# A hybrid mixer block on one core: pairs of delta tiles in 18 beats instead of 19, the first pair a beat sooner, the last tiles in another bank

## The chip, the cores and the metric

The kernel runs on one core of a Trainium2 chip. TensorE (PE) multiplies matrices into the eight banks of PSUM; VectorE (DVE), ScalarE (ACT) and GpSimd (POOL) do the rest; SyncE (SP) issues most DMAs. Each engine works off its own instructions in order and waits on semaphores that the others raise. The metric is the time of one execution in microseconds (us), the median of several runs; lower is better.

## The reference

One decoder layer of width 1024 over 1024 positions, batch 1: a modulated norm, one input projection into three causal mixers (GLA with 4 heads, mLSTM with 4 heads, gated DeltaNet with 8 heads), sigmoid merge gates, an output projection, then a modulated norm and a SwiGLU of width 2816, and a last norm. All is float32. The change is in the DeltaNet mixer, whose chunks of 64 rows need the inverse of a triangular matrix:

```python
kk = jnp.einsum('bhnid,bhnjd->bhnij', kc, kc)
a_mat = jnp.where(causal_mask(c, strict=True), beta[..., :, None] * kk * gamma, 0.0)
t_mat = a_mat + jnp.eye(c)
u = triangular_solve(t_mat, vc * beta[..., None])
w = triangular_solve(t_mat, kc * (beta * jnp.exp(cum))[..., None])
a_qk = jnp.einsum('bhnid,bhnjd->bhnij', qc, kc) * gamma
def step(state, inp):
    v_new = uu - einsum(ww, state)
    o = einsum(qd, state) + einsum(aq, v_new)
    state = state * dl[..., None, None] + einsum(ke, v_new)
    return state, o
...
y = gates[:, :, 0] * y_gla + gates[:, :, 1] * y_ml + gates[:, :, 2] * y_gdn
return y @ w_out
```

## The kernel before, in words

Every float32 product of a projection is made of three reduced-precision ones (high by high, high by low, low by high), so a block of 128 inner rows costs three matmuls. The weights are split into high and low parts on the chip: ScalarE copies the high part (`split_hi`, L1092), VectorE subtracts (`split_lo`, L1101), two halves of a weight group in two parts each.

**Beats.** The mixer section is written as a list of beats. In every beat each engine first issues what the mixers' serial chains need there and then its share of the projection. TensorE's share is called fill: the projection's matmuls of the next branch, dealt evenly over the beats of a stretch (a wide one, L179, has 512 columns and counts two; a narrow one, L171, has 256 and counts one). There are eight iterations i = 0 to 7, one per DeltaNet head. Each has a stretch p1 of B1 = 76 beats, in which DeltaNet head i is worked off while the projection of a GLA or mLSTM head runs as fill, and a stretch p2 of B2 = 42 beats, in which that GLA (i < 4) or mLSTM (i >= 4) head's eight chunks go through, five beats apart, while the projection of the next DeltaNet head runs as fill. A lead-in of 52 beats stands before, a tail of 46 (output projection as fill) in the place of the last p2.

**A pair.** The eight tiles of 128 rows of a DeltaNet head go in four pairs d, each PAIR = 19 beats long (beat j of pair d is beat 19 d + j of p1). Front (`gdn_front_pe`, `_dve`, `_act`): TensorE makes scores (part 0, L1128, bank M[0]), broadcasts the decay rows (part 1, L1141, M[1]) and transposes k and v (part 2, L1155, M[2]); VectorE adds masks (L1161), ScalarE takes exponentials (L1169). Solve (`gdn_solve_dve`, L1287 to L1291): VectorE makes the strict triangle, its first inverse blocks and their transpose. In beat j = 0 VectorE makes the attention part (L1316) and the odd tile's output (L1298). Then six levels of two beats (j = LEVEL0 = 1 to 12): a product on TensorE (L1186), a mask on VectorE (L1331), a second product (L1194), a subtraction (L1340) and a transpose (L1342), each waiting for the one before. From TILE0 = 13 six beats of state steps for two tiles (L1205 to L1220), in which the front of the next pair goes too, and its solve at j = 17. The first pair's front is in the last beats of the stretch before: TensorE in the last beats but three, VectorE's masks last but one, ScalarE and the solve in the last.

**Around it.** A chunk of GLA or mLSTM has scores (L1516 to L1521, in bank M[0], masked by VectorE at L1572 or L1575), outputs (L1531 to L1534) and a norm (L1553 to L1597). Gate tiles pass through VectorE in three stages (L1044 to L1046, L1048, L1057). `HEAD_AT`, `MOD_AT`, `MOD_SUM_AT`, `ZERO_AT` and `STATE_AT` are beats of p1 for the GLA gate's products, the modulation's sums and two clearings.

**Tail.** The output projection needs the mixers' sum transposed. `gather_pe` transposes tile t in two steps (L1853) through bank M[5], ScalarE and VectorE split it (L1880, L1897, semaphore `gt_lo`). Five tiles (`GT_INNER`) are gathered inside the last p1, tiles 5 to 7 in the tail's beats 2 to 7, since M[5] also takes the outputs of the last two delta tiles. `tail_sp` loads their rows. An output unit (`out_unit`, L968) waits for its tile's `gt_lo`; VectorE adds it to x (L981).

## Time and profile before

| | |
|---|---|
| median of 3 runs | 2774.84 us (2774.6 to 2779.07) |
| the profiled execution | 2773.6 us, span 2771.6 us |
| TensorE busy | 2660.7 us (96%) |
| TensorE weight loads | 2343.6 us (85%) |
| VectorE busy | 1902.4 us (69%) |
| ScalarE busy | 993.5 us (36%) |
| GpSimd busy | 497.2 us (18%) |

How to read it: an engine's busy time is the sum of its instructions' durations. Matmuls are pipelined and their ends are modelled, so their durations overlap, and the distance of two starts tells more than a duration. In a timeline row stand start, duration, engine, line, operation, output and inputs, and in brackets the idle time before it with what ended it. The waits view adds such times by line.

### The profile page before, as it was taken

The numbers are of one execution on the slowest core, as the hardware profiler recorded it, in microseconds if no ns is written. First come the engines' busy times: TensorE is split into PE (matmuls) and PEld (weight loads), VectorE is DVE, ScalarE is ACT, GpSimd is POOL, SyncE is SP. The second block draws the span as 40 slices with busy tenths as digits, with TensorE's granted clock in tenths as the row PEclk, the third lists the DMA queues.
The fourth block names the chain that finished last, engine by engine and source line by source line (L and its number), as shares of the span: only waits on it lengthen the run. The fifth ranks groups of instructions, "written<-read, shape, count | busy, mean of one in ns | idle before, by whom it ended". The sixth has DMA issues, their size and how long they took to land.

```text
span 2771.6 us, 44953 instructions
## 1 busy us (share of the span) xinstructions
PE 2660.7 (96%) x16632; PEld 2343.6 (85%) x16632; DVE 1902.4 (69%) x3625; ACT 993.5 (36%) x2228; POOL 497.2 (18%) x433
## 2 busy tenths in 40 slices
PE   7999999999999999999999999998999999999998
PEld 3789789889888988988998898897878888888887
DVE  4677767867877776776776775776576666666656
ACT  4633643563374364345336325333430000000002
POOL 0000410310130031000000000000043443333440
PEclk9999999999999999999999999999999999999999
DMA  6221121122122112212212212223121111111111
GB/s 204 62 58 32 43 59 47 31 66 51 20 58 67 28 41 58 49 33 67 54 30 52 57 28 58 71 64 113 33 69 54 46 54 54 46 46 46 46 46 61
DMA packets 222618, 152.44 MB, mean 55 GB/s; under 512 B 27856, under 2 KB 207032, under 8 KB 222400
## 3 DMA queue, kind: packets, MB, share of 16 engines
q1 hardware_dynamic: 209728, 141.70, 17.7%
q0 software_dynamic: 12672, 7.87, 2.9%
q8 instruction: 133, 2.18, 0.3%
q14 instruction: 85, 0.70, 0.1%
HBM read 133.28 MB, written 16.26 MB: 54 GB/s over the span
## 4 chain that ended last, share of the span: by engine, by line
PE 70%; DVE 19%; ACT 8%; issue 2%; DMA 1%; SPq 0%; DVEq 0%; ACTq 0%
PE bank L179 27%; PE bank L171 17%; PE bank L2075 8%; DVE sig L1048 2%; PE bank L1194 2%; PE bank L1186 2%; PE bank L968 2%; DVE wB_lo L1101 1%; DVE wA_lo L1101 1%; PE bank L1141 1%; PE bank L443 1%; PE bank L1128 1%; DVE feat_region L1628 1%; DVE feat_region L1342 1%; PE bank L1516 1%
## 5 line engine op out<-in xcount | busy, mean ns | idle before, releaser
L171 PE MATMUL bank<-wB_hi,h_hi 128*128 128x256 f32 x1024 | 301.2, 294 | 4.4 <-ACT feat_region L1005 2.7
L171 PE MATMUL bank<-wA_hi,h_hi 128*128 128x256 f32 x1024 | 297.6, 291 | 4.6 <-ACT feat_region L1005 2.7
L171 PE MATMUL bank<-wB_lo,h_hi 128*128 128x256 f32 x1024 | 300.5, 293 | 0.0
L171 PE MATMUL bank<-wB_hi,h_lo 128*128 128x256 f32 x1024 | 300.1, 293 | 0.0
L171 PE MATMUL bank<-wA_lo,h_hi 128*128 128x256 f32 x1024 | 296.9, 290 | 0.0
L171 PE MATMUL bank<-wA_hi,h_lo 128*128 128x256 f32 x1024 | 296.8, 290 | 0.0
L179 PE MATMUL bank<-h_hi,wA_hi 128*128 128x512 f32 x672 | 267.4, 398 | 2.7 <-DVE feat_region L981 2.2
L179 PE MATMUL bank<-h_hi,wA_lo 128*128 128x512 f32 x672 | 267.5, 398 | 0.0
L179 PE MATMUL bank<-h_hi,wB_hi 128*128 128x512 f32 x672 | 267.4, 398 | 0.0
L179 PE MATMUL bank<-h_hi,wB_lo 128*128 128x512 f32 x672 | 267.3, 398 | 0.0
L179 PE MATMUL bank<-h_lo,wA_hi 128*128 128x512 f32 x672 | 266.5, 397 | 0.0
L179 PE MATMUL bank<-h_lo,wB_hi 128*128 128x512 f32 x672 | 266.3, 396 | 0.0
L2188 POOL DMA_DIRECT2D y_scratch<-ybuf x56 | 48.1, 859 | 935.3 <-DVE ybuf L1298 935.3
L171 PEld LDWEIGHTS bank<-wB_hi,h_hi 128*128 128x128 f32 x1024 | 199.4, 195 | 7.9 <-ACT feat_region L1005 3.1
L171 PEld LDWEIGHTS bank<-wA_hi,h_hi 128*128 128x128 f32 x1024 | 195.9, 191 | 8.3 <-ACT feat_region L1005 3.1
L171 PEld LDWEIGHTS bank<-wB_hi,h_lo 128*128 128x128 f32 x1024 | 199.3, 195 | 1.2 <-issue 0.7
L171 PEld LDWEIGHTS bank<-wB_lo,h_hi 128*128 128x128 f32 x1024 | 199.1, 194 | 1.0 <-issue 0.7
L171 PEld LDWEIGHTS bank<-wA_hi,h_lo 128*128 128x128 f32 x1024 | 195.7, 191 | 1.1 <-issue 0.7
L171 PEld LDWEIGHTS bank<-wA_lo,h_hi 128*128 128x128 f32 x1024 | 195.6, 191 | 0.9 <-issue 0.7
L1048 DVE RECIPROCAL sig<-sig 128x128 f32<-128x128 f32 x192 | 183.0, 953 | 6.6
L2132 DVE TENSOR_TENSOR feat_region<-feat_region,bank 128x512 f32<-128x512 f32 x176 | 121.1, 688 | 83.2 <-PE bank L2075 80.9
L2091 ACT ACTIVATE conv_in<-bank 128x512 f32<-128x512 f32 x44 | 26.3, 598 | 356.4 <-PE bank L179 356.3
(395 smaller groups left out, 6232.9 us busy)
## 6 DMA issues: line engine op xcount, KB each, us to landing
w_raw<-in_w_in_dram SPq DMA_DIRECT2D x96, 512.0 KB, 3.8
w_raw<-in_w_ffn_up_dram SPq DMA_DIRECT2D x44, 512.0 KB, 3.8
rows_region<-in_ada_w_dram SPq DMA_DIRECT2D x64, 256.0 KB, 2.7
w_raw<-in_w_ffn_down_dram SPq DMA_DIRECT2D x22, 512.0 KB, 3.5
rows_region<-in_x_dram SPq DMA_DIRECT2D x8, 512.0 KB, 7.6
w_raw<-in_w_in_dram SPq DMA_DIRECT2D x16, 256.0 KB, 2.9
y_scratch<-ybuf SPq DMA_DIRECT2D x32, 128.0 KB, 1.9
y_scratch<-ybuf POOLq DMA_DIRECT2D x32, 128.0 KB, 3.1
```

Of the source, the lines that this page charges most:

```text
L171: mm = nc.tensor.matmul(bank[:, n_out:n_out + n1 - n0], (h_hi, h_lo)[hp][:, k, t * P:t * P + P], buf[wp][:, k, n0:n1], start=(s == 0), sto ...
L179: mm = nc.tensor.matmul(bank[0:n, :], buf[wp][:, k, n0:n0 + n], (h_hi, h_lo)[hp][:, k, half * HALF:half * HALF + HALF], start=(s == 0), st ...
L443: mm = nc.tensor.matmul(bank[0:1, 0:ADA_W], c_act[:, k:k + 1], ada_ring[slot][:, k], start=(k == 0), stop=(k == KT - 1))
L968: mm = nc.tensor.matmul(G[u % 2][:, 0:256], (h_hi, h_lo)[hp][:, k, cols], (A_W, B_W)[g % 2][wp][:, k], start=(s == 0), stop=(s == n_steps( ...
L1048: step(dve.reciprocal(ex, ex), "sig_recip")
L1101: step(dve.tensor_tensor(lo, raw, hi.bitcast(F32), ALU.subtract), "w_lo")
L1128: last = mm(M[0][:, c * 256:c * 256 + 256], kq[:, 0, t:t + P], kq[:, :, t:t + P], start=True, stop=True)
L1186: last = mm(M[3][:, c * 64:c * 64 + 64], at[:, c, 0:P], one(xm[:, c], b, 0), start=True, stop=True)
L1194: last = mm(M[3][:, 256 + c * 64:320 + c * 64], pm[:, v, c], one(xmt[:, c], b, 1), start=True, stop=True)
L2075: mm = nc.tensor.matmul(DOWN[n % 4][:], hid[hp][:, k, t * P:t * P + P], D_W[wp][:, k, half * HALF:half * HALF + HALF], start=(s == 0), sto ...
L2132: step(dve.tensor_tensor(acc, acc, DOWN[n % 4][:], ALU.add), "down_read")
L2188: pool.dma_start(y_dram[t * P:t * P + P, i * P:i * P + P], ybuf[:, t % 2, 0:P], accum_op=ALU.add).then_inc(sem(f"y_add{t % 2}"), 16)
```

## The change

A pair takes 18 beats: LEVEL0 is 0, so the levels begin in beat 0 and the state steps in beat 12, and p1 has 72 beats instead of 76. The same fill is dealt over them: beats of 10 or 11 narrow matmuls instead of mostly 10, of 5 or 6 wide ones instead of mostly 5. What VectorE did in beat 0 ahead of everything now stands behind the first level's mask. The first pair's front begins at `FRONT0` = 37 of p2's 42 beats, one sooner on TensorE, VectorE and ScalarE; its solve stays in the last beat. The outputs of the last two delta tiles go through bank M[2] (`out_bank`); for that the last head's first chunk scores wait until all delta outputs are read. Six tiles are gathered inside the last p1, in its beats 57 to 69 before the tail's start (15 to 3 beats ahead of it), and the last two in the tail's beats 2 to 5. The other tables follow the shorter p1.

```diff
--- before.py
+++ after.py
@@ -747,7 +747,7 @@
     mod_acc = kt_sub[:, 1, 2:6].rearrange("p a n -> p (a n)")
     mod_row = mod_ring[0:1, 0]
     MOD_AT = [6 + 4 * k for k in range(KT)]
-    MOD_SUM_AT = (43, 46)
+    MOD_SUM_AT = (42, 45)
 
     def mod_part(i):
         part, half = 2 + i // 2, i % 2
@@ -830,7 +830,7 @@
 
 
     N_IT = GDN_H
-    B1, B2, PAIR, CHUNK2, TAIL = 76, 42, 19, 5, 46
+    B1, B2, PAIR, CHUNK2, TAIL = 72, 42, 18, 5, 46
     LB = 52
     BEATS = LB + N_IT * (B1 + B2) - B2 + TAIL + 1
 
@@ -1109,8 +1109,9 @@
 
     PAIRS = NT // 2
 
-    LEVEL0 = 1
+    LEVEL0 = 0
     TILE0 = LEVEL0 + 2 * len(LEVELS)
+    FRONT0 = B2 - 5
 
     def gdn_front_pe(pe, i, d, part):
 
@@ -1167,6 +1168,10 @@
         for c in range(2):
             t = 2 * d + c
             step(nc.scalar.activation(wts[:, c], wts[:, c], ACT.Exp, bias=gq[:, 2, t:t + 1]), "gdn_e" if c else None)
+
+    def out_bank(T):
+
+        return M[2 if T >= NT * N_IT - 2 else 5][:, 0:P]
 
     def gdn_pe(pe, i, d, j):
         mm = nc.tensor.matmul
@@ -1211,12 +1216,10 @@
             else:
                 if T:
                     pe.wait_ge(sem("gdn_y"), T)
-                if T == NT * N_IT - 2:
-                    pe.wait_ge(sem("gt_lo"), 2 * GT_INNER)
                 pe.wait_ge(sem("gdn_qd"), D_ + 1)
-                mm(M[5][:, 0:P], qdec[:, c], state_d[:], start=True, stop=False)
+                mm(out_bank(T), qdec[:, c], state_d[:], start=True, stop=False)
                 pe.wait_ge(sem("gdn_vv"), T + 1)
-                mm(M[5][:, 0:P], at[:, c, P:2 * P], vnew[:], start=False, stop=True)
+                mm(out_bank(T), at[:, c, P:2 * P], vnew[:], start=False, stop=True)
                 mm(M[4][:, 2 * P:3 * P], kend[:, c], vnew[:], start=True, stop=True).then_inc(sem("gdn_os"), 1)
 
     def gdn_act(act, step, i, d, j):
@@ -1249,7 +1252,7 @@
                     act.wait_ge(sem("gdn_y"), T)
                 if T % NT == 0 and i:
                     act.wait_ge(sem("g_y"), NT * i)
-                step(A(junk[:, 0:P], M[5][:, 0:P], ACT.Square, accum_out=rs[:, 0:1]))
+                step(A(junk[:, 0:P], out_bank(T), ACT.Square, accum_out=rs[:, 0:1]))
                 step(A(rs[:, 1:2], rs[:, 0:1], ACT.Ln, scale=1.0 / GDN_DV, bias=eps[:]))
                 step(A(rs[:, 2:3], rs[:, 1:2], ACT.Exp, scale=-0.5), "gdn_rms")
 
@@ -1295,7 +1298,7 @@
         dve.wait_ge(sem("gdn_rms"), T + 1)
         dve.wait_ge(sem("sig_used"), gate_no[GDN[i - 1] + 6 + t] + 1)
         y_free(dve, 2 * NT * i + t)
-        step(dve.scalar_tensor_tensor(ybuf[:, t % 2, 0:P], M[5][:, 0:P], rs[:, 2:3], gdn_m[:, t], ALU.mult, ALU.mult),
+        step(dve.scalar_tensor_tensor(ybuf[:, t % 2, 0:P], out_bank(T), rs[:, 2:3], gdn_m[:, t], ALU.mult, ALU.mult),
              "gdn_y")
 
     def gdn_dve(dve, step, i, d, j):
@@ -1308,16 +1311,7 @@
             gdn_solve_dve(dve, step, i, d + 1)
         if j == TILE0 + 3:
             gdn_out_dve(dve, step, i, 2 * d)
-        if j == 0:
-            if d == 0:
-                step(dve.memset(state_d[:], 0.0), "gdn_s")
-            if D_:
-                dve.wait_ge(sem("gdn_os"), 2 * D_)
-            step(tt(at[:, :, P:2 * P], M[0][:].rearrange("p (c n) -> p c n", c=2)[:, :, P:2 * P], wts[:, :, P:2 * P],
-                    ALU.mult), "gdn_at")
-            if d:
-                gdn_out_dve(dve, step, i, 2 * d - 1)
-        elif LEVEL0 <= j < TILE0:
+        if LEVEL0 <= j < TILE0:
             v, phase = divmod(j - LEVEL0, 2)
             b = LEVELS[v]
             n = 64 // b
@@ -1329,6 +1323,15 @@
                 dve.wait_ge(sem("gdn_p"), 6 * D_ + v + 1)
                 mask = level_mask[:, v].rearrange("p (n b) -> p n b", b=b).unsqueeze(1).broadcast_to([P, 2, n, b])
                 step(tt(pair(pm[:, v], b, 0), cols(0), mask, ALU.mult), "gdn_pm")
+                if v == 0:
+                    if d == 0:
+                        step(dve.memset(state_d[:], 0.0), "gdn_s")
+                    if D_:
+                        dve.wait_ge(sem("gdn_os"), 2 * D_)
+                    step(tt(at[:, :, P:2 * P], M[0][:].rearrange("p (c n) -> p c n", c=2)[:, :, P:2 * P],
+                            wts[:, :, P:2 * P], ALU.mult), "gdn_at")
+                    if d:
+                        gdn_out_dve(dve, step, i, 2 * d - 1)
                 if v == 2:
                     dve.wait_ge(sem("gdn_eq"), D_ + 1)
                     step(tt(qdec[:], qdec[:], kq[:, 1, 2 * d * P:2 * (d + 1) * P].rearrange("p (c t) -> p c t", c=2),
@@ -1354,8 +1357,8 @@
                      "gdn_s")
 
 
-    HEAD_AT = [6, 10, 25, 29]
-    ZERO_AT, STATE_AT = 60, 66
+    HEAD_AT = [6, 10, 24, 28]
+    ZERO_AT, STATE_AT = 57, 62
 
     def head_pe(pe, i, r):
         if branch(i) == "gla" and r in HEAD_AT:
@@ -1503,6 +1506,8 @@
                 pe.wait_ge(sem("gdn_at"), PAIRS * (i + 1))
                 pe.wait_ge(sem("gdn_eq"), PAIRS * (i + 1))
                 pe.wait_ge(sem("gdn_kv"), PAIRS * (i + 1))
+                if i == N_IT - 1:
+                    pe.wait_ge(sem("gdn_y"), NT * N_IT)
             if C:
                 pe.wait_ge(sem("g_scd"), C)
                 pe.wait_ge(sem("g_kend"), C)
@@ -1768,13 +1773,13 @@
 
 
     P2_LAST = p2(N_IT - 1)
-    GT_INNER = 5
+    GT_INNER = 6
     GT_AT = {}
     for t in range(NT):
         u = next(u for u in range(N_UNITS) if units[u][1:] == ("rg", t, N_IT - 1, 1))
         b = max(unit_done[u] + 1, max(GT_AT.values(), default=0) + 1, 0 if t < GT_INNER else P2_LAST + 2)
         GT_AT.update({(t, 0): b, (t, 1): b + 1})
-    assert GT_AT[GT_INNER - 1, 1] < P2_LAST - 4
+    assert GT_AT[GT_INNER - 1, 1] < P2_LAST
     O2_DONE = [unit_done[unit_of("o2", t)] for t in range(NT)]
     NRM0 = O2_DONE[3] + 4
     NRM_AT = [NRM0 + o for o in (0, 2, 3, 4, 5, 6, 7, 8)]
@@ -1846,7 +1851,7 @@
                     n = 2 * t + q
                     if q == 0:
                         pe.wait_ge(sem(f"gt_in{t % 2}"), gt_loaded(t))
-                    pe.wait_ge(sem("gdn_y"), NT * N_IT - (2 if t < GT_INNER else 0))
+                    pe.wait_ge(sem("gdn_y"), NT * N_IT - 2)
                     if n:
                         pe.wait_ge(sem("gt_lo"), n)
                     for j, k in enumerate(range(4 * q, min(4 * q + 4, EARLY_K))):
@@ -2219,8 +2224,8 @@
                     ml_prep_pe(pe, *at_)
                 if r2 is not None and i < N_IT - 1:
                     conv_pe(pe, i, r2)
-                    if r2 >= B2 - 4 and r2 < B2 - 1:
-                        gdn_front_pe(pe, i + 1, 0, r2 - (B2 - 4))
+                    if FRONT0 <= r2 < FRONT0 + 3:
+                        gdn_front_pe(pe, i + 1, 0, r2 - FRONT0)
                 tail_pe(pe, b)
                 for u, s0, s1 in fill[b]:
                     fill_unit(pe, u, s0, s1)
@@ -2260,7 +2265,7 @@
                 if r2 is not None and i < N_IT - 1:
                     gates_act(act, step, i, r2)
                     conv_act(act, step, i, r2)
-                    if r2 == B2 - 1:
+                    if r2 == FRONT0 + 3:
                         gdn_front_act(act, step, i + 1, 0)
                 tail_act(act, step, b)
                 if r1 is not None:
@@ -2301,7 +2306,7 @@
                 if r2 is not None and i < N_IT - 1:
                     gates_dve(dve, step, i, r2)
                     conv_dve(dve, step, i, r2)
-                    if r2 == B2 - 2:
+                    if r2 == FRONT0 + 2:
                         gdn_front_dve(dve, step, i + 1, 0)
                     if r2 == B2 - 1:
                         gdn_solve_dve(dve, step, i + 1, 0)
```


On VectorE, at the start of DeltaNet head 1 (pair 0), the end of the solve and the first level stood like this; `feat_region` holds the triangle and the level's operands, `bank` the product, `state_d` the delta state:

```order
L1290 TENSOR_TENSOR feat_region<-feat_region,ident 128x256
L1291 STREAM_TRANSPOSE feat_region<-feat_region 128x256
L1313 MEMSET state_d 128x128
L1316 TENSOR_TENSOR feat_region<-bank,feat_region 128x2x128
L1331 TENSOR_TENSOR feat_region<-bank,level_mask 128x64x2
L1101 TENSOR_TENSOR wB_lo<-w_raw,wB_hi 128x4x128
L1340 TENSOR_TENSOR feat_region<-feat_region,bank 128x64x2
L1342 STREAM_TRANSPOSE feat_region<-feat_region 128x256
```

and now, with the line numbers of the changed kernel (L1325 is the level's mask, L1331 the attention part, L1343 and L1345 subtraction and transpose):

```order
L1293 TENSOR_TENSOR feat_region<-feat_region,ident 128x256
L1294 STREAM_TRANSPOSE feat_region<-feat_region 128x256
L1325 TENSOR_TENSOR feat_region<-bank,level_mask 128x64x2
L1328 MEMSET state_d 128x128
L1331 TENSOR_TENSOR feat_region<-bank,feat_region 128x2x128
L1343 TENSOR_TENSOR feat_region<-feat_region,bank 128x64x2
L1345 STREAM_TRANSPOSE feat_region<-feat_region 128x256
L1101 TENSOR_TENSOR wB_lo<-w_raw,wB_hi 128x4x128
```

The level's mask has moved ahead of the state's clearing and the attention part, and the first weight split behind the level's transpose.

On VectorE, between the state steps of pair 0 and the first level of pair 1 of the same head, before (`sig` is a gate tile in work, `rows_region` here the modulation's sum, `ybuf` the output row):

```order
L1048 RECIPROCAL sig<-sig 128x128
L1287 TENSOR_TENSOR feat_region<-bank,feat_region 128x2x128
L1289 TENSOR_TENSOR xmt<-feat_region,pair_mask 128x256
L1290 TENSOR_TENSOR xmt<-xmt,ident 128x256
L1291 STREAM_TRANSPOSE feat_region<-xmt 128x256
L1057 TENSOR_TENSOR feat_region<-feat_region,sig 128x128
L1353 SCALAR_TENSOR_TENSOR state_d<-state_d,gex,bank 128x128
L811 SCALAR_TENSOR_TENSOR rows_region<-rows_region,c_act 128x512
L1316 TENSOR_TENSOR feat_region<-bank,feat_region 128x2x128
L1298 SCALAR_TENSOR_TENSOR ybuf<-bank,rs,feat_region 128x128
L1044 TENSOR_TENSOR feat_region<-rows_region,gain_d 128x128
```

and now:

```order
L1290 TENSOR_TENSOR feat_region<-bank,feat_region 128x2x128
L1292 TENSOR_TENSOR xmt<-feat_region,pair_mask 128x256
L1293 TENSOR_TENSOR xmt<-xmt,ident 128x256
L1294 STREAM_TRANSPOSE feat_region<-xmt 128x256
L1048 RECIPROCAL sig<-sig 128x128
L1356 SCALAR_TENSOR_TENSOR state_d<-state_d,gex,bank 128x128
L1057 TENSOR_TENSOR feat_region<-feat_region,sig 128x128
L1325 TENSOR_TENSOR feat_region<-bank,level_mask 128x64x2
L1331 TENSOR_TENSOR feat_region<-bank,feat_region 128x2x128
L1301 SCALAR_TENSOR_TENSOR ybuf<-bank,rs,feat_region 128x128
L811 SCALAR_TENSOR_TENSOR rows_region<-rows_region,c_act 128x512
L1343 TENSOR_TENSOR xmt<-xmt,bank 128x64x2
```

The solve has moved ahead of the gate tile's reciprocal (L1048), and the level's mask with its subtraction and transpose ahead of the next gate tile.

On TensorE the last fill of p2 is dealt as before, but the first pair's scores (L1128, now L1129) follow the last chunk's scores after 12 fill matmuls instead of 23, and between the transposes (L1155, now L1156) and the first level product stand 34 fill matmuls, with the last chunk's outputs directly ahead of the transposes.

## Rows read from the trace of the kernel before

**Rows 1.** The page: busy time of an engine, share of the span, instructions

```profile
PE 2660.7 (96%) x16632; PEld 2343.6 (85%) x16632; DVE 1902.4 (69%) x3625; ACT 993.5 (36%) x2228; POOL 497.2 (18%) x433
```

**Rows 2.** Waits of TensorE: line, what it waited for, us in total, times, longest

```profile
PE bank L1186 <- DVE feat_region L1342: 13.9, 26, 0.9
```

**Rows 3.** Timeline of TensorE, end of p2(1): start, duration, instruction

```profile
372.45 0.59 PE L1531 MATMUL bank<-rows_region,sc 128*128 128x256 f32 x2
...
373.75 1.05 PE L1141 MATMUL bank<-ident,gq 128*128 128x128 f32 x8
...
375.83 0.29 PE L171 MATMUL bank<-wB_hi,h_hi 128*128 128x256 f32 x1
375.96 0.60 PE L1155 MATMUL bank<-ident,feat_region 128*128 128x128 f32 x4
...
380.31 0.55 PE L1186 MATMUL bank<-feat_region 128*128 128x64 f32 x4
...
381.91 0.56 PE L1194 MATMUL bank<-feat_region 128*128 128x64 f32 x4
```

**Rows 4.** Timeline of ScalarE, the same stretch

```profile
376.08 0.38 ACT L1012 ACTIVATE rows_region<-bank 128x256 f32<-128x256 f32 x1 [1.05 <-PE bank L171]
376.50 1.05 ACT L1169 ACTIVATE feat_region<-feat_region,gq 128x256 f32<-128x256 f32 x2
```

**Rows 5.** Timeline of VectorE, the same stretch

```profile
379.02 0.45 DVE L1291 STREAM_TRANSPOSE feat_region<-feat_region 128x256 f32<-128x256 f32 x1
```

**Rows 6.** Timeline of TensorE, ends of p2(4) and p2(5), mLSTM heads

```profile
1287.69 0.27 PE L1521 MATMUL bank<-ident,rows_region 128*128 128x128 f32 x1
...
1509.27 0.27 PE L1521 MATMUL bank<-ident,rows_region 128*128 128x128 f32 x1
...
1515.79 0.59 PE L1531 MATMUL bank<-rows_region,sc 128*128 128x257 f32 x2
```

**Rows 7.** Timeline of VectorE, the same two stretches

```profile
1290.04 0.29 DVE L1575 TENSOR_TENSOR sc<-bank,dq 128x128 f32<-128x128 f32 x1
...
1513.02 0.29 DVE L1575 TENSOR_TENSOR sc<-bank,dq 128x128 f32<-128x128 f32 x1
...
1522.45 0.45 DVE L1291 STREAM_TRANSPOSE feat_region<-feat_region 128x256 f32<-128x256 f32 x1
```

**Rows 8.** Timeline of VectorE, levels of pair 0 of p1(1)

```profile
386.13 0.29 DVE L1340 TENSOR_TENSOR feat_region<-feat_region,bank 128x128 f32<-128x128 f32 x1
386.46 0.45 DVE L1342 STREAM_TRANSPOSE feat_region<-feat_region 128x256 f32<-128x256 f32 x1
386.94 0.95 DVE L1048 RECIPROCAL sig<-sig 128x128 f32<-128x128 f32 x1
387.92 0.69 DVE L1101 TENSOR_TENSOR wB_lo<-w_raw,wB_hi 128x512 fp32r<-128x512 f32 x1
```

**Rows 9.** Timeline of TensorE, level products of pairs 0, 1 and 3 of p1(1)

```profile
388.99 0.66 PE L1194 MATMUL bank<-feat_region 128*128 128x64 f32 x4 [0.17 <-DVE feat_region L1331]
...
415.26 0.55 PE L1186 MATMUL bank<-feat_region 128*128 128x64 f32 x4
...
427.75 0.55 PE L1186 MATMUL bank<-feat_region 128*128 128x64 f32 x4
...
486.51 0.55 PE L1186 MATMUL bank<-feat_region 128*128 128x64 f32 x4
...
502.05 0.55 PE L1194 MATMUL bank<-xmt,feat_region 128*128 128x64 f32 x4
```

**Rows 10.** Timeline of TensorE, tail

```profile
1922.71 0.63 PE L1853 MATMUL bank<-ident,sig 128*128 128x128 f32 x4 [2.49 <-DVE h_lo L1897]
...
1928.60 0.36 PE L968 MATMUL bank<-wA_hi,h_hi 128*128 128x256 f32 x1 [1.45 <-DVE h_lo L1897]
```

**Rows 11.** Timeline of VectorE, tail

```profile
1895.15 0.35 DVE L1298 SCALAR_TENSOR_TENSOR ybuf<-bank,rs,feat_region 128x128 f32<-128x128 f32 x1
```

**Rows 12.** Busy us by stretch: PE, PEld, DVE, ACT, POOL, granted clock, DMA share, GB/s

```profile
1912.30:1918.00 5.70, 5.68 (x27) 5.70 (x28) 1.11 (x2) 0.60 (x1) 0.00 (x0) 0.50 1.04 406
```

## The prediction

> **What bounds the kernel now.** I read the page's busy shares first, then TensorE's waits, then the timeline of a few places. TensorE is busy 96% of the span and VectorE 69% [rows 1]. The change adds and removes no matmul, so TensorE's work stays, and the time can move only by the idle stretches between its instructions. The largest group inside the triangle levels is the level product that waits for VectorE's transpose: 26 waits, 13.9 us [rows 2]. Such a number understates: a matmul's end is modelled, so I measure a loss from start to start against an undisturbed beat.
>
> An undisturbed beat: two starts of one beat in pair 0, with five wide matmuls, lie 1.60 us apart (380.31 and 381.91) [rows 3]. Narrow matmuls follow each other at 0.12 us (375.83 to 375.96, nearer 0.119 over many) [rows 3]; ten of them and the level product give 1.63. After the change most beats hold 10 or 11 instead of 10, on the mean 0.56 matmul or 0.07 us more, and there are four beats fewer: the same work, dealt differently.
>
> **Handover between heads (p2 to p1).** The front of the first pair goes a beat sooner in TensorE's order, and its first level product too (beat 0 instead of 1). VectorE's and ScalarE's own order there is unchanged but for the mask product, so the question is whether their chain is ready a beat earlier.
>
> GLA heads. From the last chunk output (L1531, 372.45) TensorE has the three products 1.30 (to 373.75), the transposes 0.35 (L1155; the row broadcasts L1141 now stand a beat before), 0.08 of re-entry and 11 narrow matmuls 1.31: 3.04. The unit that ScalarE evicts ends two matmuls before that, so eviction starts at 3.17, as 376.08 stood 0.25 behind 375.83 [rows 3, 4]. Exponentials start 0.42 later (376.08 to 376.50) [rows 4], and from there to the end of the solve's transpose it is 379.02 + 0.45 - 376.50 = 2.97 [rows 4, 5]. The product may start at 3.17 + 0.42 + 2.97 + 0.05 = 6.61. TensorE's own path is 3.04 + 23 x 0.119 = 5.78. Loss 0.83; before, the product stood at 7.86 (380.31 - 372.45) and nothing was lost. It occurs behind the lead-in, whose chain ends in the same eviction, and behind the four GLA heads: 5 x 0.83 = +4.1.
>
> mLSTM heads. Their chain is the chunk's denominator on VectorE and ScalarE: from L1531 (1515.79) to the end of the transpose (1522.45 + 0.45) 7.11 [rows 6, 7]. Against 5.78 + the wake-up of 0.05: 1.38 x 3 = +4.1.
>
> The moved score products L1128 wait for bank M[0], which the last chunk's score mask (L1575) must have read. In head 6 TensorE would reach them at 1509.27 + 0.11 + 12 x 0.119 = 1510.8, L1575 ends at 1513.31 [rows 6, 7]: a 2.5 us stall. Before, they started at about the same time, 1513.4, but with that beat's 11 matmuls (1.31) already done, which now come after: net +1.26. In heads 5 and 7: 1287.69 + 1.54 = 1289.2 against 1290.33 [rows 6, 7], +1.15 each. Sum +3.6. In the GLA heads the mask is done 0.8 before. Queued behind a stalled L1128 are only TensorE's own fills; VectorE meanwhile works off conv and gates.
>
> **Levels in p1.** The weight splits (L1101) stand where they stood, at the quarter points of p1, which are the pairs' starts both before and after. But the levels begin a beat sooner, so VectorE has one beat less between solve and the split work. I walk VectorE's queue in the new order with durations from rows: level subtraction 0.29, transpose 0.45, reciprocal 0.95, split 0.69, each + 0.03 [rows 8]; a product reaches VectorE 0.66 after it starts. The same walk over the old order gives the old starts of pair 0 to 0.05.
> - Pair 0, from the start of beat 0. TensorE alone reaches beat 6 after 32 wide matmuls and six products, 32 x 0.233 + 6 x 0.44 = 10.1 (5 x 0.233 + 0.44 is the 1.60). VectorE: beat 3's product reaches it at 5.7; subtraction and transpose to 6.5, three small products of a gate tile 0.9, a split 0.7: 8.1; beat 4's mask 8.4, a decay product 0.45, the reciprocal 0.98, a split 0.72: 10.6; beat 5's subtraction and transpose 0.8: 11.4. Loss 1.3. Before: 388.99 - 381.91 = 7.08 for four beats of 1.6, loss about 0.65 [rows 3, 9]. +0.65 x 8 = +5.2.
> - Pair 1: before, 427.75 - 415.26 = 12.49 for six level beats with a gate product of 0.65, nominal 10.43, loss 2.06 [rows 9]; by the walk 1.7 after (solve no longer behind the reciprocal, mask ahead of the attention product). In mLSTM heads 2.56 to 1.65 by the same walk. -0.35 x 4 - 0.9 x 4 = -5.0.
> - Pair 2: +0.2 x 8 = +1.6.
> - Pair 3, where VectorE is full: before 502.05 - 486.51 = 15.54 for seven beats of 1.63, loss 4.1 [rows 9]; after 3.4 in the levels and 0.3 less in the state steps. -1.05 x 4 - 0.3 x 3 = -5.1; the last head 0, since its scaled weights (L1071) fill what is freed.
>
> Moving the attention mask behind the level mask, the later ZERO_AT, STATE_AT, HEAD_AT and the modulation sums cost 0: same durations, hidden in VectorE's beat; if that cover is missing it is inside the bounds of the levels.
>
> **Tail.** The last delta tiles go to bank M[2], so tile 5's gather moves ahead of the tail. The tail then lacks the gathers at its beats 6 and 7: the waits of 2.49 and 1.45 [rows 10] and 0.3 + 0.6 of their drains go, -4.8. The load of tile 7 is still issued where it was, which gives back about 0.5: -4.3. The new wait of the first score product on all outputs finds the last one done at 1895.15 + 0.35 [rows 11], just ahead of TensorE: 0, at worst +0.4. Eight inner gathers now stand in eight successive beats, each waiting for the last one's split: +1.0 (0 to 2.5).
>
> **Clock.** In the 5.7 us after the tail's 3.3 us wait the granted clock is 0.50, 1.2 GHz [rows 12]; the 2.5 us stall of head 6 is the one new wait of that size, +1.4 (0 to 3).
>
> **Sum.** 4.1 + 4.1 + 3.6 + 5.2 + 1.6 - 5.0 - 5.1 - 4.3 + 1.0 + 1.4 = +6.6 us. The profiled execution took 2773.6; 2780.2 for its kind, and the median is 1.2 above it: 2781.4. Bounds: the handovers (11.8) follow from rows to about 2; the level terms are a difference of walks, -3.3 in sum, each head good to 0.7 at best, so -9 to +4; tail -5 to 0.
>
> **Rivals.**
> - Even: the levels gain 5 more than I walked, because the longer beats let VectorE catch up at every pair. For it: the beats are longer by 0.07 each, 48 level beats and 3.4 us a head, far more than the 0.6 a head it takes. Against: at pair 3 VectorE is full, and what TensorE has more to do there it has less elsewhere. 2776.
> - Faster: the level waits vanish. Then about 2 x 8 us more of loss goes from pairs 1 and 3, handovers stay. -14: 2761 to 2767, I take 2765. For it: the 13.9 us [rows 2] are waits for exactly these levels. Against it: the walk shows pair 0 losing more, not less.
> - Much slower: the handover stalls throw the clock. Place: the first level product of every head and L1128 of three; price 1.4 us of half-rate matmuls each; it decides as soon as waits of 0.8 to 1.4 us are enough. 7 to 8 times: +11 more, 2792. For it the half clock behind the 3.3 us wait [rows 12]; against it that the level waits of before, under 1 us, leave the beats behind them at full rate. [...]
> - The change doesn't shorten the tail: another 4 slower, inside the range.
>
> **Chances.** Forecast (2776 to 2788) 0.50, even 0.25, faster 0.15, much slower 0.10. A measurement of this kernel can tell 0.2% (5.5 us) from no change: slower above 2780.4. Of the forecast's half some three quarters lie above: slower 0.37 + 0.10 = 0.47; same 0.13 + 0.25 + 0.02 = 0.40; faster 0.13. Range 2767 to 2790, leaving out the best of the faster case and the clock case.
>
> **What would show it.** Right: the first L1191 (the old L1186) of each head waits 0.6 to 1.4 for VectorE; L1129 waits 1 to 2.5 in three heads; the first pair's fourth level waits about 1; two L1853-like waits of the tail are gone; p1 of GLA heads is unchanged within 1 us. Wrong: p1 stretches shorter by over 2 us each, or no wait at the first level, which would mean that ScalarE's exponentials came a beat sooner.

## The result, and the profile after

| | before | after |
|---|---|---|
| median of 5 runs | 2774.60 us (2771.8 to 2779.07) | 2790.47 us (2789.55 to 2797.25) |
| ratio, 95% interval | | 1.0059 (1.0048 to 1.0070) |
| profiled execution, its span | 2773.6, 2771.6 us | 2789.56, 2787.7 us |

The change makes the kernel 16 us slower; +6.6 was forecast and 2790 was the upper end of the range, so the sign was right, the size not, and the median lies just outside. The work of every engine is what it was [rows 1]. TensorE's busy time even fell by 2.4 us, and the mean granted clock of the execution is 0.987 in both, so the 16.1 us between the two spans are, taken together, idle time of TensorE. One of the eleven executions of a kernel further down (splits five beats later in the kernel before) took 3180 us at a mean granted clock of 0.77 and is left out of its ratio.

```profile
PE 2658.3 (95%) x16632; PEld 2343.7 (84%) x16632; DVE 1902.3 (68%) x3625; ACT 994.0 (36%) x2228; POOL 498.7 (18%) x433
```

The waits of TensorE in the changed kernel (line, what it waited for, us in total, times, longest); L1191 and L1199 are the level's two products, L1294 is the transpose of the solve and L1345 that of a level:

```profile
PE bank L1191 <- DVE feat_region L1345: 35.0, 58, 2.0
...
PE bank L1191 <- DVE feat_region L1294: 7.2, 8, 1.3
...
PE bank L1858 <- DMA sig<-y_scratch: 4.3, 1, 4.3
...
PE bank L1199 <- DVE feat_region L1325: 3.7, 10, 1.0
...
PE bank L1129 <- issue: 1.7, 3, 0.6
```

The wait for a level's transpose was 13.9 us in 26 waits [rows 2] and is 35.0 in 58, while the wait for a level's mask (8.3 us before) is 3.7. Behind the solve stand 7.2 us that did not exist.

Waits do not give the loss by themselves, so I cut both traces at the same events, the first level product of each pair and the chunk outputs, and compared the stretches. Two stretches don't hold the same work: the first level product stands a beat sooner, so 1.2 us of fill (10.1 matmuls of 0.119) moved from the handover into p1, and the row broadcasts (0.87) moved from the handover into p2. With that taken off (the 1.2 of a head ends up in pair 3's stretch, since pairs 0 to 2 hold the same fill in both kernels):

| stretch | forecast | measured |
|---|---|---|
| handover, first level product, 8 heads | +8.2 | +8.3 |
| p2 with the moved score products | +3.6 | +0.4 |
| pair 0, 8 heads | +5.2 | +5.7, and +3.1 at half clock in heads 0 and 2 |
| pair 1, 8 heads | -5.0 | +2.1 |
| pair 2, 8 heads | +1.6 | +2.4 |
| pair 3, heads 0 to 6 | -5.1 | -2.7 |
| pair 3 of head 7, with the inner gathers | +1.0 | +1.0 |
| tail | -4.3 | -4.3 |
| clock elsewhere | +1.4 | not apart from the noise |
| sum | +6.6 | +16.0 |

In sum the miss is that of two rows, pairs 1 and 3: a gain of 10.1 was forecast, and together they gave 0.6. The other rows miss too, by up to 3.6 us, but these misses cancel (p2 3.2 less than forecast, pair 0 3.6 more, 3.1 of it by the clock).

The handover in the changed kernel, TensorE, start of p1(1) (start, duration, instruction, in brackets the wait):

```profile
376.47 0.59 PE L1536 MATMUL bank<-rows_region,sc 128*128 128x256 f32 x2
...
383.12 0.63 PE L1191 MATMUL bank<-feat_region 128*128 128x64 f32 x4 [0.69 <-DVE feat_region L1294]
```

and the same in an mLSTM head, p1(6):

```profile
1532.23 0.59 PE L1536 MATMUL bank<-rows_region,sc 128*128 128x257 f32 x2
...
1539.44 0.63 PE L1191 MATMUL bank<-feat_region 128*128 128x64 f32 x4 [1.24 <-DVE feat_region L1294]
```

From the last chunk output to the level product it is 6.65 us, where 6.61 was forecast, and 7.21, where 7.16 was [rows 3 to 7].

### The profile page after: what moved, and what is told of

It is laid out like the page before. It is cut to its first block, busy times and chain, and to the rows that moved or that the text cites. A ratio compares the mean times of both kernels' runs of the same rounds, so it can differ in the third digit from the quotient of the medians.

```text
span 2787.7 us, 44953 instructions
## 1 busy us (share of the span) xinstructions
PE 2658.3 (95%) x16632; PEld 2343.7 (84%) x16632; DVE 1902.3 (68%) x3625; ACT 994.0 (36%) x2228; POOL 498.7 (18%) x433
## 4 chain that ended last, share of the span: by engine, by line
PE 70%; DVE 18%; ACT 9%; issue 2%; DMA 1%; SPq 0%; DVEq 0%; ACTq 0%
PE bank L179 27%; PE bank L171 17%; PE bank L2080 8%; PE bank L1191 2%; DVE sig L1048 2%; PE bank L968 2%; PE bank L1199 2%; DVE wB_lo L1101 1%; DVE wA_lo L1101 1%; PE bank L1142 1%; PE bank L1129 1%; PE bank L443 1%; DVE feat_region L1345 1%; DVE feat_region L1633 1%; PE bank L1536 1%
## 5 line engine op out<-in xcount | busy, mean ns | idle before, releaser
L179 PE MATMUL bank<-h_hi,wA_hi 128*128 128x512 f32 x672 | 266.7, 397 | 2.3 <-DVE feat_region L981 1.9
L179 PE MATMUL bank<-h_hi,wB_lo 128*128 128x512 f32 x672 | 267.8, 399 | 0.0
L179 PE MATMUL bank<-h_hi,wB_hi 128*128 128x512 f32 x672 | 267.7, 398 | 0.0
L179 PE MATMUL bank<-h_lo,wB_hi 128*128 128x512 f32 x672 | 266.9, 397 | 0.0
L179 PE MATMUL bank<-h_hi,wA_lo 128*128 128x512 f32 x672 | 266.4, 396 | 0.0
L179 PE MATMUL bank<-h_lo,wA_hi 128*128 128x512 f32 x672 | 265.9, 396 | 0.0
L1048 DVE RECIPROCAL sig<-sig 128x128 f32<-128x128 f32 x192 | 183.0, 953 | 6.6
L1191 PEld LDWEIGHTS bank<-feat_region 128*128 128x128 f32 x768 | 103.3, 190 | 62.4 <-DVE feat_region L1345 50.6
```

The lines of the kernel that those rows point to most:

```text
L179: mm = nc.tensor.matmul(bank[0:n, :], buf[wp][:, k, n0:n0 + n], (h_hi, h_lo)[hp][:, k, half * HALF:half * HALF + HALF], start=(s == 0), st ...
L1048: step(dve.reciprocal(ex, ex), "sig_recip")
L1191: last = mm(M[3][:, c * 64:c * 64 + 64], at[:, c, 0:P], one(xm[:, c], b, 0), start=True, stop=True)
```

## The experiments

All ratios are to the kernel before on the same chip, with 95% intervals. "us" of a ratio means its distance from one times 2775. The traces show one execution each. "A stretch" is measured between first level products, and "the splits" are VectorE's subtractions L1101 of p1 together with ScalarE's copies L1092 ahead of them.

### The tail part alone

```diff
+    def out_bank(T):
+        return M[2 if T >= NT * N_IT - 2 else 5][:, 0:P]
...
-                if T == NT * N_IT - 2:
-                    pe.wait_ge(sem("gt_lo"), 2 * GT_INNER)
...
+                if i == N_IT - 1:
+                    pe.wait_ge(sem("gdn_y"), NT * N_IT)
...
-    GT_INNER = 5
+    GT_INNER = 6
```

(shortened: the products and reads of the delta outputs use `out_bank(T)`, and all gathers wait for the same number of outputs)

> The kernel before (pairs of 19 beats, front where it was) with the tail part of the change alone: last two delta tiles in bank M[2], six tiles gathered inside the last p1. Theory 1 (the tail term was right): the tail loses its waits of 2.49 and 1.45 us, the inner gathers cost about 1, so 3 to 4 us faster than before, and everything ahead of the last p1 unchanged to 0.5 us. Theory 2 (the gathers only move their waits into the last p1, whose levels already wait): within 1 us of before. If theory 1 holds, the rest of the change costs about 20 us by itself.

Ratio 0.9988 (0.9979 to 0.9997), -3.3 us, median 2772.69: the net of the tail terms was right, and the rest of the change costs about 20 us. The mechanism was only half right. In the changed kernel the two waits of [rows 10] are gone, but a longer one stands in their place. The trace puts it down to the load of tile 7, which was left where it was:

```profile
1925.65 0.41 PE L1858 MATMUL bank<-ident,feat_region 128*128 128x128 f32 x2 [2.29 <-DVE h_lo L1902]
...
1933.67 0.66 PE L1858 MATMUL bank<-ident,sig 128*128 128x128 f32 x4 [4.29 <-DMA sig<-y_scratch]
```

I had priced that at 0.5 us. The load is only the last 1.1 us of it: the split of the gather before (L1902) ended at 1932.56 and the load at 1933.6. With the tail part alone the same transpose waits 3.33 us for that split (L1901 there), and the load has landed 0.3 us sooner. ScalarE's copy for that split stands behind the norm of a chunk, a place that I had not looked at. TensorE's waits from the last delta output to the last gather fell from 10.5 us before to 6.9 with the tail part alone and 8.0 in the changed kernel. By stretches the tail of this run became 8.0 us shorter and head 7's last pair, with the inner gathers, 2.7 longer; forecast were 4.3 and 1.0. The net was right because the two misses are opposite.

### The front a beat sooner, alone

```diff
+    FRONT0 = B2 - 5
...
-                    if r2 >= B2 - 4 and r2 < B2 - 1:
-                        gdn_front_pe(pe, i + 1, 0, r2 - (B2 - 4))
+                    if FRONT0 <= r2 < FRONT0 + 3:
+                        gdn_front_pe(pe, i + 1, 0, r2 - FRONT0)
```

(the same for ScalarE and VectorE)

> The kernel before with the first pair's front one beat sooner (beat 37 of p2) and nothing else; the first level product stays in beat 1. Theory 1 (in the changed kernel p2 costs nothing of its own once the moved broadcasts of 1.05 us are counted where they now stand): within 1.5 us of before. Theory 2 (as forecast: the moved score products stall for the last mLSTM chunk's mask): 3.6 us slower, with waits of 1.1 to 2.5 us on L1128 in three heads.

Ratio 1.0025 (1.0015 to 1.0034), +6.9 us: theory 1 falls, the sooner front costs by itself. The waits of L1129 are 1.04, 1.06 and 1.06, a little under the lower end of what was forecast, and make 3.2 us:

```profile
PE bank L1129 <- issue: 3.2, 3, 1.1
```

The rest is 0.23 us at the first level product of the mLSTM heads, and p2 of those heads, which took 76.9 to 77.1 us against 72.5 to 74.9 before (0.87 of it the moved broadcasts). Part of that is the clock: over these three stretches the mean granted clock is 0.91, 0.91 and 0.91 here, 0.93 in each in the changed kernel, and 0.95, 0.93 and 0.91 before. So the row "p2: +0.4" above is no evidence that the sooner front is free; its falls of the clock differ from one execution to the next (last section) by more than the term.

### The weight splits five beats later, in the changed kernel

```diff
         b0 = after[g - 2] if g >= 2 else 8 * g
+        if b0 >= LB and (b0 - LB) % (B1 + B2) < B1 - 12 and g < OUT0:
+            b0 += 5
```

> The changed kernel with the weight splits of p1 (ScalarE's copies and VectorE's subtractions L1101) and the loads behind them five beats later, so that they stand in beats 6 to 10 of a pair and no longer in 1 to 4. Theory 1 (VectorE's amount of work in the first level beats sets TensorE's pace there): of the 38.7 us that level products wait for L1345 and L1325, at least a third goes, 10 to 16 us faster than the changed kernel, pair 0 without the wait of 1.10 us and without the half clock behind it in heads 0 and 2. Theory 2 (the levels' chain of product, mask, product, subtraction, transpose is itself as long as the beats): same time to 3 us. The handover waits of 0.69 and 1.25 us stay under both.

Ratio 1.0019 (1.0004 to 1.0034) against 1.0059, so about 11 us back: theory 1. The largest level waits:

```profile
PE bank L1191 <- DVE feat_region L1345: 11.1, 21, 2.0
...
PE bank L1191 <- DVE feat_region L1294: 7.2, 8, 1.2
...
PE bank L1191 <- DVE xmt L1343: 5.1, 11, 0.6
...
PE bank L1191 <- DVE feat_region L1343: 3.8, 8, 0.6
```

New waits, for the subtraction L1343 of later levels, came with the new place: all waits for L1345, L1343 and L1325 together fell from 38.7 to 23.8 us. Pair 0's fourth level waits for nothing now, and the handover waits stayed, as expected. The gain stands in the first two pairs (table in "The splits one beat later"): pair 1 took 12 us less over the eight heads and pair 0 7 less, pair 2 took 3.5 more and pair 3 2.5 more. The runs of this kernel lay far apart (2772 to 2792); the profiled one is at the low end.

### The same in the kernel before

The same edit.

> The kernel before with the same move of the weight splits by five beats. Theory 1 (VectorE's amount of work in the first level beats): the 22.2 us of level waits fall by at least a third, 5 to 10 us faster than before. Theory 2 (the chain itself): same to 2 us.

Ratio 1.0019 (1.0010 to 1.0028): 5 us slower, so neither theory holds as I put it. The waits of the first levels went, new ones came in the fifth level of every pair. Pairs 1 and 3 became 5.3 us shorter over the eight heads, pairs 0 and 2 14.0 longer:

```profile
PE bank L1186 <- DVE feat_region L1342: 16.6, 31, 1.0
...
PE bank L1194 <- DVE feat_region L1331: 10.1, 16, 2.8
```

"VectorE's amount of work" is thus too coarse. What counts is which instructions of a level the splits stand in front of.

### One spare beat at the start of p1

```diff
-    B1, B2, PAIR, CHUNK2, TAIL = 72, 42, 18, 5, 46
+    B1, B2, PAIR, CHUNK2, TAIL = 73, 42, 18, 5, 46
...
-    FRONT0 = B2 - 5
+    FRONT0 = B2 - 4
...
-                    gdn_pe(pe, i, *divmod(r1, PAIR))
+                    if r1:
+                        gdn_pe(pe, i, *divmod(r1 - 1, PAIR))
```

(the same for VectorE and ScalarE, and the tables of beats one later)

> The changed kernel with one spare beat at the start of p1 (73 beats): pair 0's levels begin in beat 1, the first pair's front stands where it stood before the change, all pairs still take 18 beats; the tail part stays. Theory 1 (the handover costs what its waits say): the waits of 0.69 and 1.25 us on the first level product go in all eight heads, 8 to 9 us faster than the changed kernel, ratio to before about 1.003. Theory 2 (what is not waited for there is waited for at the fourth level of pair 0, since VectorE is behind): within 3 us of the changed kernel, and the wait of 1.10 us grows.

Ratio 1.0026 (1.0016 to 1.0037), 9 us faster than the changed kernel: theory 1. The waits for L1294 are gone, and so is pair 0's wait of 1.10, against theory 2. But the 9 us are a net sum. Between the two traces, with the fill taken off as above, the handovers (8.3) and pair 0 (10.5, with 3.1 of half clock) came back, while pair 3 lost 7, and in pair 1 of every head a wait appeared that no other kernel here has:

```profile
PE bank L171 <- ACT rows_region L999: 7.0, 8, 1.0
```

It is for a fill bank that ScalarE evicts, and ScalarE's copy for a split stands just ahead of that eviction (L1092, 1.06 us, 422.23 to 423.29 in head 1). So the 10.5 us that part this kernel from the one with the tail part (0.9988) are not the levels of pairs 1 to 3 alone.

### The spare beat and the splits five beats later

> The one spare beat together with the weight splits of p1 five beats later. Theory 1 (handover and the splits' place in the first levels are two separate costs that add): 8 to 9 us faster than the changed kernel for the spare beat and 8 to 10 for the splits, together near 2773, ratio to before 0.998 to 1.000. Theory 2 (they are one cost seen twice): no faster than the better of the two alone, ratio 1.002 to 1.003.

Ratio 0.9979 (0.9969 to 0.9988), median 2771.95, just under theory 1's range: the two gains add. The wait for L999 is gone with it, so up to 7.0 of the 13 us that the later splits win here are ScalarE's and not the levels'. It is gone with the splits three and eight beats later too.

### The modulation's sums elsewhere

```diff
-    MOD_AT = [6 + 4 * k for k in range(KT)]
+    MOD_AT = [6, 9, 12, 15, 24, 27, 30, 33]
```

> The changed kernel with the modulation's eight sums (0.5 to 0.75 us each on VectorE) at beats 6, 9, 12, 15, 24, 27, 30, 33 instead of 6, 10, 14, 18, 22, 26, 30, 34, so that none falls into beats 0 to 5 of pair 1. Theory 1 (my walk of pair 1 failed because the sum of beat 18 now stands ahead of the first level's subtraction, where before it stood in beat 22 of 19 + 3): pair 1's level beats 0 to 6 lose at least 0.7 us less in each of the eight heads, 5 to 8 us faster than the changed kernel. Theory 2 (VectorE is full there with or without that sum): within 2 us of it.

Ratio 1.0053 (1.0038 to 1.0069), no difference from the changed kernel that can be measured, as theory 2 has it (the two intervals leave room for up to 7 us). The trace says more: pair 1's stretch became 0.8 us shorter in the GLA heads (36.15 against 36.92) and 0.2 in the mLSTM heads, 4 us in all, but behind pair 0's wait of 1.10 us the clock now fell in all four GLA heads and no longer in two, and each fall costs 1.6. So the sum of beat 18 had some part in pair 1's loss, 4 us where theory 1 had 5 to 8, and the clock took most of it back; the wait for L1345 is still 29.9 us, and that for L1325 rose from 3.7 to 8.1.

### Pairs of 19 beats with the levels a beat sooner

The kernel before with LEVEL0 = 0, the level's mask ahead of the attention product, the front as in the changed kernel, the tail part.

> Pairs of 19 beats as before, but with the levels beginning in beat 0, the state steps in beat 12, the spare beat at the end of a pair, the level's mask ahead of the attention product, the front as in the changed kernel, and the tail part. Against the changed kernel only the dealing (76 beats instead of 72) differs. Theory 1 (the shorter pair costs by itself, since the same VectorE work has a beat less between solve and levels): pairs 1 to 3 lose about 1 us a head less each than in the changed kernel, 8 to 12 us faster than it, ratio 1.002. Theory 2 (the earlier levels of pair 0 and the handover are all of the cost): within 3 us of the changed kernel.

Ratio 1.0104 (1.0091 to 1.0117), median 2803.96: slower than the changed kernel by 12 us. Theory 1 falls entirely, and theory 2 did not foresee this either. With all 76 beats, so with no shorter pair, the level waits are there:

```profile
PE bank L1191 <- DVE feat_region L1345: 31.9, 41, 2.0
```

In the mLSTM heads p1 lasts 142.8 to 143.2 us, as in the changed kernel (143.2 to 143.5). What the GLA heads lose beyond it (2.5 us a head in the last stretch before the chunks, where L1210 now waits 7.4 us for L1356 and L179 4.1 for L1020) I did not follow up.

### The splits one beat later in the kernel before

The edit with b0 += 1.

> The kernel before with the weight splits of p1 one beat later, nothing else: the four split instructions of VectorE then stand in the second to fifth beat of the levels, as in the changed kernel, and no longer in the first to fourth. Theory 1 (the changed kernel's levels lose because its levels begin at the pair's start and the splits so fall one level beat deeper, behind the second product's subtraction and onto the decay product of the fourth beat): pair 0 gets a wait of about 1.1 us at its fourth level and the half clock behind it in some heads, pairs 1 and 3 lose about 0.5 more, together 5 to 10 us slower than before, without any shorter pair. Theory 2 (the shorter pair is what costs): within 2 us of before.

Ratio 1.0026 (1.0016 to 1.0036), +7.3 us: theory 1 by the time. Where the loss stands is another matter. Pair 1 of head 5, TensorE: the product of the fourth level (seventh level beat) waits 1.07, where it waited 0.34 before:

```profile
1346.43 0.66 PE L1194 MATMUL bank<-xmt,feat_region 128*128 128x64 f32 x4
...
1349.41 0.66 PE L1186 MATMUL bank<-feat_region 128*128 128x64 f32 x4 [1.07 <-DVE feat_region L1342]
```

and VectorE in that stretch:

```profile
1346.09 0.29 DVE L1331 TENSOR_TENSOR feat_region<-bank,level_mask 128x128 f32<-128x128 f32 x1
1346.41 0.43 DVE L1334 TENSOR_TENSOR feat_region<-feat_region 128x256 f32<-128x256 f32 x1
1346.87 0.95 DVE L1048 RECIPROCAL sig<-sig 128x128 f32<-128x128 f32 x1
1347.86 0.69 DVE L1101 TENSOR_TENSOR wA_lo<-w_raw,wA_hi 128x512 fp32r<-128x512 f32 x1
1348.59 0.29 DVE L1340 TENSOR_TENSOR xmt<-xmt,bank 128x128 f32<-128x128 f32 x1
1348.91 0.45 DVE L1342 STREAM_TRANSPOSE feat_region<-xmt 128x256 f32<-128x256 f32 x1
```

A product reaches VectorE 0.66 us after its start, so that of 1346.43 could be subtracted from 1347.09 on. The decay product and the reciprocal, which stood there before as well, and now the last split too, hold VectorE until 1348.59. I expected the wait in pair 0 too; there it came in the mLSTM heads (0.44) and not in the GLA heads (0.17, unchanged).

But pair 1 as a whole lost nothing by this. The split that now holds up the third level no longer holds up the first, and the wait of the second level's product behind it, 0.62 in the kernel before, is gone. The fourth level's product starts 12.24 us after the first one's in both kernels. The kernel before:

```profile
1338.28 0.66 PE L1186 MATMUL bank<-feat_region 128*128 128x64 f32 x4 [0.62 <-DVE feat_region L1342]
```

The same holds in pair 3. The loss stands in pairs 0 and 2, where no product waited for the split of the first level, so that nothing was won there. Over the eight heads, against the kernel before (us, one execution each; pair 3 up to the first chunk output, and less the 9.6 of moved fill in the two kernels made from the changed one; the forecast's +1.0 of inner gathers is in pair 3):

| | pair 0 | pair 1 | pair 2 | pair 3 | sum |
|---|---|---|---|---|---|
| forecast of the changed kernel | +5.2 | -5.0 | +1.6 | -4.1 | -2.3 |
| changed kernel | +8.8 | +2.1 | +2.5 | -1.6 | +11.7 |
| changed, splits 5 later | +1.8 | -9.9 | +6.0 | +0.8 | -1.2 |
| before, splits 1 later | +3.3 | -0.4 | +4.4 | -0.4 | +6.9 |
| before, splits 5 later | +3.9 | -2.5 | +10.2 | -2.8 | +8.7 |

So this run shows that one beat between splits and levels costs 7 us in the kernel before. It does not show why the forecast gain of pairs 1 and 3 failed to come; for pair 1 the run that shows it is the changed kernel with the splits five beats later.

The length of p1 from its first level product to the first chunk output (us; the changed kernel less the 1.2 of moved fill) agrees between the shift alone and the change, but by the table above this is a likeness of sums, not of pairs:

| kernel | p1(1), GLA | p1(3), GLA | p1(4) | p1(5) | p1(6) |
|---|---|---|---|---|---|
| before | 148.7 | 148.1 | 140.9 | 140.9 | 141.2 |
| splits 1 later | 149.4 | 148.6 | 142.0 | 141.9 | 142.9 |
| changed | 149.5 | 149.0 | 142.0 | 142.0 | 142.3 |
| one spare beat | 149.4 | 149.0 | 142.1 | 141.7 | 142.3 |
| one spare beat, splits 8 later | 147.1 | 147.7 | 137.3 | 137.3 | 137.8 |

(In the last row heads 1 and 3 have a fall of the clock in pair 3; heads 0 and 2 have none and took 145.4 and 145.0.) With one spare beat and the splits eight beats later, pair 3 of the mLSTM heads takes 38.2 us instead of 39.8, so its levels too hang on where the splits stand.

### The splits three and eight beats later

The one spare beat with b0 += 3 and with b0 += 8.

> The kernel with one spare beat at the start of p1, 18-beat pairs and the tail part, the splits three beats later instead of five: they stand in beats 4 to 7. Theory 1 (any place behind the first four level beats, where state steps, output, modulation and gate tile meet, is good): ratio to before 0.997 to 0.999, as with five. Theory 2 (beats 4 and 5, with the decay product and the reciprocal, are the full ones): 1.000 to 1.003.

Ratio 0.9966 (0.9953 to 0.9978), median 2765.8, theory 1 and a little better than its range, though waits are left at the fourth level (0.36 to 0.95).

> The same with the splits eight beats later, in beats 9 to 12, where the last levels and the first state steps are. Theory 1 (VectorE has room there: with five beats the waits left are on L1353 and the last levels' masks at beats 9 and 10): ratio 0.996 to 0.998. Theory 2 (the state steps' chain from L1210 over L1353 to L1356 is then what waits): 0.999 to 1.002.

Ratio 0.9919 (0.9905 to 0.9932), median 2754.09 (2751.77 to 2755.1): 22 us faster than the kernel before and 39 faster than the changed one. Better than either theory had it. The level waits are all but gone. What is left stands in pair 3's state steps, which waited 5.6 us before and are now held up by the late splits (in head 1 one ends at 508.66, L1353 starts at 508.70):

```profile
PE bank L1215 <- DVE feat_region L1353: 15.1, 7, 3.3
...
PE bank L1191 <- DVE feat_region L1345: 6.2, 13, 1.9
```

### Is the shorter pair worth anything then?

The kernel before with the tail part and b0 += 9: the same place relative to the levels, pairs of 19 beats.

> Pairs of 19 beats with the levels from beat 1 (as before the change), with the tail part, and the weight splits of p1 nine beats later, which is the same place relative to the levels as in the kernel with one spare beat and splits eight beats later (0.9919 of before). The only difference between the two is the pair's length, 19 or 18 beats. Theory 1 (with the splits out of the levels nothing waits there, and the same fill dealt over fewer, longer beats is worth little): ratio 0.991 to 0.994, within 4 us of the other. Theory 2 (the longer beats of the 18-beat pair give VectorE the time to follow): 0.995 or more, 8 us or more slower than the other.

Ratio 0.9951 (0.9938 to 0.9965), median 2760.97. The intervals are apart, 9 us lie between the two: theory 2 by the time. With the splits out of the way, the change as a whole is a gain. With them in it, it was a loss. That the pair's length alone makes the 9 us is not shown: contrary to what I expected, the two kernels also differ in VectorE's order, since the kernel with 18 beats has the level's mask ahead of the attention part and the delta output, and the other one has not. Pairs of 19 beats with the new order and late splits were not run. Where the 9 us lie I can say only in part: p1 is 0.7 to 1.3 us a head shorter in the mLSTM heads and 4 shorter with the tail in head 7; the rest is not apart from the clock's falls.

## Why the prediction was wrong

**Handover: right.** Against TensorE's own path of 5.78 us the 6.65 and 7.21 are losses of 0.87 and 1.43, where 0.83 and 1.38 were forecast. The stretches give +8.3 for the row, forecast +8.2. The 9 us that the spare beat gave back are no second measurement of it, being a net of several terms.

**Score products L1128: mechanism right, price open.** The waits were 0.54, 0.56 and 0.56, not 1.15 to 2.5. TensorE came there 1.70 us behind the last chunk's scores, forecast 1.54, but the mask ended 2.16 behind them, where I had taken 2.64 and 4.04 from the kernel before. VectorE reaches the mask through four small instructions of the chunk before, and these waited 2.27 us for ScalarE in head 6 before and 0.28 in the changed kernel. With the sooner front alone the mask ended 2.64 to 2.66 behind, and the waits were 1.04 to 1.06. The 2.5 us stall of head 6 appeared nowhere. Alone, the sooner front cost 7 us; forecast were 3.6.

**Pair 0: right** but for the clock, and by the chain that I walked. VectorE, in p1(1) of the changed kernel:

```profile
391.35 0.29 DVE L1325 TENSOR_TENSOR feat_region<-bank,level_mask 128x128 f32<-128x128 f32 x1
391.67 0.42 DVE L1337 TENSOR_TENSOR feat_region<-feat_region 128x256 f32<-128x256 f32 x1
392.13 0.95 DVE L1048 RECIPROCAL sig<-sig 128x128 f32<-128x128 f32 x1
393.12 0.69 DVE L1101 TENSOR_TENSOR wB_lo<-w_raw,wB_hi 128x512 fp32r<-128x512 f32 x1
393.84 0.29 DVE L1343 TENSOR_TENSOR feat_region<-feat_region,bank 128x128 f32<-128x128 f32 x1
394.16 0.45 DVE L1345 STREAM_TRANSPOSE feat_region<-feat_region 128x256 f32<-128x256 f32 x1
```

and TensorE behind it: the wait that was forecast as about 1.3 is 1.10.

```profile
391.69 0.66 PE L1199 MATMUL bank<-feat_region 128*128 128x64 f32 x4
...
394.66 0.66 PE L1191 MATMUL bank<-feat_region 128*128 128x64 f32 x4 [1.10 <-DVE feat_region L1345]
```

**Pairs 1 and 3: the step that failed**, "by the walk 1.7 after" with -5.0 for pair 1, and "after 3.4 in the levels and 0.3 less in the state steps" with -5.1 for pair 3. I had written that the splits stay at the quarter points while the levels begin a beat sooner, and carried that through for pair 0 only. For pairs 1 and 3 I counted what the new order saves (the solve ahead of the reciprocal, the mask ahead of the attention product; it did save, the second level's wait in pair 1 fell from 0.61 to 0.24) and not what the later place of the splits costs in the second and third level. The forecast loss of pair 1 was 1.7 us after 2.06; it stayed at the old length in the mLSTM heads and grew by 0.5 in the GLA heads. The first level did gain, 0.5 to 0.6 us. The second lost more: it takes 4.61 us in the GLA head shown and 4.65 in head 5, before 3.69 and 3.70, because reciprocal and split, which stood together ahead of the first level's subtraction, now stand together ahead of the second's. Ahead of the third one's stand the modulation's sum and the last split. In pair 1 of p1(1):

```profile
424.59 0.95 DVE L1048 RECIPROCAL sig<-sig 128x128 f32<-128x128 f32 x1
425.58 0.69 DVE L1101 TENSOR_TENSOR wA_lo<-w_raw,wA_hi 128x512 fp32r<-128x512 f32 x1
426.31 0.29 DVE L1343 TENSOR_TENSOR xmt<-xmt,bank 128x128 f32<-128x128 f32 x1
...
428.94 0.75 DVE L811 SCALAR_TENSOR_TENSOR rows_region<-rows_region,c_act 128x512 f32<-128x512 f32 x1
429.73 0.69 DVE L1101 TENSOR_TENSOR wA_lo<-w_raw,wA_hi 128x512 fp32r<-128x512 f32 x1
430.46 0.29 DVE L1343 TENSOR_TENSOR xmt<-xmt,bank 128x128 f32<-128x128 f32 x1
```

TensorE in the same stretch of the changed kernel:

```profile
422.52 0.66 PE L1191 MATMUL bank<-feat_region 128*128 128x64 f32 x4 [0.24 <-DVE feat_region L1345]
...
427.13 0.66 PE L1191 MATMUL bank<-feat_region 128*128 128x64 f32 x4 [0.51 <-DVE feat_region L1345]
...
431.28 0.66 PE L1191 MATMUL bank<-feat_region 128*128 128x64 f32 x4 [0.50 <-DVE feat_region L1345]
```

and in the kernel before, whose third and fourth levels of this pair (423.28, 427.75) wait for nothing worth naming:

```profile
419.59 0.66 PE L1186 MATMUL bank<-feat_region 128*128 128x64 f32 x4 [0.61 <-DVE feat_region L1342]
...
423.28 0.66 PE L1186 MATMUL bank<-feat_region 128*128 128x64 f32 x4
```

Two waits of 0.5 and one of 0.24 took the place of one of 0.61. In pair 3 it is alike: the first level gained 0.55 in head 1 and 0.25 in head 5, the second lost 0.64 and 0.59. With the splits five beats later the second level takes 3.62 us and the third 3.39 in both pairs, and pair 1 gives 9.9 us over the eight heads, more than the 5.0 forecast. So for pair 1 it is shown that the splits' place took the forecast gain. In pair 3 that run gives nothing back in sum, since the splits then hold up its later levels; there the cause is shown for the second and third level and argued for the whole. That the reciprocal alone would have done no harm was not tried.

**Tail: right in its net** (-3.3 by itself; -4.3 forecast for the tail and +1.0 for the inner gathers), in part by luck: by stretches the two were -8.0 and +2.7 in the run with the tail part alone, and what waits afterwards was not foreseen.

**Clock: wrong place.** 1.4 forecast for the stall of head 6, which did not come; the clock fell elsewhere, behind pair 0's wait of 1.10, in two of eight heads, 3.1 us. Over the whole execution nothing of it is left, since the mean granted clock is the same in both.

**The rivals.** "Faster, the level waits vanish" was argued away by the walk of pair 0, rightly for this kernel. Something like it, and more, happens when the splits move. "Much slower by the clock", 2792, came out at nearly the right time by a wrong mechanism: the levels, not the clock, made the difference. Its place was wrong too: behind the first level product of heads 1 to 7, which waited 0.69 to 1.25 us, the granted clock is 1.00 in each.

## What to carry to other kernels

When a serial chain is moved by a beat against work that is placed by another table, walk the chain again in every place where the two meet, level by level, not only in the first. When a run's total matches the change that it is to explain, compare the two stretch by stretch before you call it the cause. If a bulk instruction (here a 0.69 us split that has most of a quarter of p1 to be done in) can stand anywhere in a wide stretch, put it where the chain has ended: moving it eight beats was worth 30 us in the kernel with the spare beat, up to 7 of them ScalarE's, and more than all else here. A change that loses may be sound and badly placed, so look at what the loss stands behind before you undo it.
